# Dilated attention scores as three single-rate products of split queries and keys, on each head's own 64 rows, two heads interleaved

## The reference

```python
def dilated_attention(q, k, v, positions):
    h = N_HEADS_C
    q = partial_rope_2(to_heads(q, h), positions)
    k = partial_rope_2(to_heads(k, h), positions)
    v = to_heads(v, h)
    outs, lses = [], []
    for window, dil in DILATED_PATTERNS:
        o, lse = dilated_branch(q, k, v, window, dil)
        outs.append(o)
        lses.append(lse)
    wts = jax.nn.softmax(jnp.stack(lses, axis=0), axis=0)
    o = jnp.sum(wts[..., None] * jnp.stack(outs, axis=0), axis=0)
    return from_heads(o)
```

## Time and profile before

| | us |
|---|---|
| median of 3 runs | 2215.31 |
| lowest, highest | 2212.41, 2215.72 |
| profiled execution, its own time | 2214.59 |
| its span (first to last instruction) | 2212.8 |

### The profile page before, as it was taken

How to read it: one execution, slowest core, us unless ns; L and a number is a source line. 1 busy time by engine, 2 the same in 40 slices (tenths; PEclk the granted TensorE clock), 3 DMA queues, 4 the chain that set the end, 5 groups by cost and what they waited for, 6 DMA issues and landing times.

```text
span 2212.8 us, 33023 instructions
## 1 busy us (share of the span) xinstructions
PE 2160.8 (98%) x12331; PEld 1840.0 (83%) x12331; DVE 1500.5 (68%) x2224; ACT 944.2 (43%) x1882; POOL 1189.3 (54%) x582
## 2 busy tenths in 40 slices
PE   6999999999999999999999999999999999999997
PEld 4788888877899988887887898888897887888885
DVE  6834877554666692897646776677896728777676
ACT  3254663011556610644743555412555725455311
POOL 4747403776477677745016644577653037444673
PEclk9999999999999999999999999999999999999999
DMA  8422102422133333232002222322221012222221
GB/s 318 156 73 86 62 30 88 181 94 96 58 115 115 109 142 135 77 115 77 1 4 92 96 91 100 115 95 84 107 93 61 1 39 86 92 90 115 95 95 57
DMA packets 32776, 206.78 MB, mean 93 GB/s; under 512 B 4080, under 2 KB 4336, under 8 KB 11632
## 3 DMA queue, kind: packets, MB, share of 16 engines
q1 hardware_dynamic: 32192, 200.27, 24.9%
q10 hardware_dynamic: 432, 4.46, 0.5%
HBM read 202.61 MB, written 2.10 MB: 93 GB/s over the span
## 4 chain that ended last, share of the span: by engine, by line
PE 87%; DVE 8%; DMA 1%; DVEq 1%; issue 1%; ACT 1%; POOL 1%; POOLq 0%; SPq 0%; ACTq 0%
PE PS L1118 18%; PE PS L1120 18%; PE PS L1119 18%; PE PS L1560 5%; PE PS L1572 5%; PE PS L1375 3%; PE PS L1373 3%; PE PS L1374 3%; PE PS L1586 3%; PE PS L1449 2%; PE PS L1451 2%; PE PS L1450 2%; DMA raw<-slabs_dram 1%; DVE PS L3374 1%; PE PS L1132 1%
## 5 line engine op out<-in xcount | busy, mean ns | idle before, releaser
L665 POOL TENSOR_TENSOR w_hi<-raw,zero_c 128x512 fp32r<-128x512 f32 (+1 forms) x135 | 279.5, 2088 | 546.2 <-PE PS L1120 544.8
L669 POOL TENSOR_TENSOR w_lo<-raw,w_hi 128x512 fp32r<-128x512 f32 (+1 forms) x135 | 367.4, 2740 | 5.8
L1118 PE MATMUL PS<-b_hi,w_hi 128*128 128x512 f32 x528 | 209.8, 397 | 1.0 <-POOL w_lo L888 1.0
L1119 PE MATMUL PS<-b_lo,w_hi 128*128 128x512 f32 x528 | 209.3, 396 | 0.0
L1120 PE MATMUL PS<-b_hi,w_lo 128*128 128x512 f32 x528 | 209.3, 396 | 0.0
L3288 DVE TENSOR_TENSOR b_lo<-a_all,b_hi 128x512 fp32r<-128x512 f32 x44 | 162.5, 3732 | 49.4 <-ACT b_hi L2446 49.4
L1118 PE MATMUL PS<-f_hi,w_hi 128*128 128x512 f32 x448 | 177.6, 397 | 0.7 <-DVE f_lo L2590 0.7
L1120 PE MATMUL PS<-f_hi,w_lo 128*128 128x512 f32 x448 | 177.6, 396 | 0.0
L1119 PE MATMUL PS<-f_lo,w_hi 128*128 128x512 f32 x448 | 177.6, 396 | 0.0
L688 POOL TENSOR_TENSOR w_lo<-raw,w_hi 128x512 fp32r<-128x512 f32 x48 | 71.0, 1479 | 93.6 <-ACT w_hi L2438 93.6
L1118 PEld LDWEIGHTS PS<-b_hi,w_hi 128*128 128x128 f32 x528 | 99.5, 188 | 25.6 <-POOL w_lo L888 1.2
(11 more groups left out here) (570 smaller groups left out, 6822.3 us busy)
## 6 DMA issues: line engine op xcount, KB each, us to landing
raw<-slabs_dram SPq DMA_DIRECT2D x161, 1024.0 KB, 4.8
aux<-ada_dram SPq DMA_DIRECT2D x18, 512.0 KB, 5.0
ada_first<-ada_dram SPq DMA_DIRECT2D x11, 512.0 KB, 13.9
cmpw<-cmpw_dram ACTq DMA_DIRECT2D x2, 2048.0 KB, 11.7
ada_late<-ada_dram SPq DMA_DIRECT2D x8, 512.0 KB, 3.3
ada_last<-ada_dram SPq DMA_DIRECT2D x8, 512.0 KB, 5.8
xT<-xT_dram SPq DMA_DIRECT2D x1, 2048.0 KB, 9.2
out_dram<-t SPq DMA_DIRECT2D x4, 512.0 KB, 2.7
```

The lines of the kernel that those rows point to most:

```text
L665: high = nc.gpsimd.tensor_tensor(w_hi[:, slot, c], raw[:, slot, c], zero[:, 0:c.stop - c.start], ALU.add)
L669: low = nc.gpsimd.tensor_tensor(w_lo[:, slot, c], raw[:, slot, c], w_hi[:, slot, c].bitcast(f32), ALU.subtract)
L1118: nc.tensor.matmul(out, a_hi_, b_hi_, start=start, stop=False)
L1119: nc.tensor.matmul(out, a_hi_, b_lo_, start=False, stop=False)
```

## The change

The queries of two heads are now one transposed tile without zeros, kept as high and low part (`T2_split`), and so are the keys (high part in `T2a`, low part in `z2_split`, over the keys' own place). A job names the 64 rows that are its own (`rows`). Three single-rate products of 64 rows (high x high, high x low, low x high) give a score tile. Two heads that share a tile (`mate`) take their score tiles together: at an even step TensorE issues six matmuls, head A and head B by turns, into two banks, and at the odd step none. Tiles of one key block are computed 256 columns wide (`wide = max(2, nb)`); the second half is not read. The two heads' outputs lie side by side in one bank and are divided together, after the second one's last product (`finishes`). In the eight turns at steps 3 to 38 ScalarE now takes the high part and VectorE, in the same step, the low part, which waits for ScalarE's (`turned_act`). The high parts of the outputs lie in two places instead of one (`o_high`).

```diff
@@ -353,8 +353,10 @@
         t4 = at("t4", 81920, [P, KD + 1, SEQ])
+        z2_split = at("z2_split", 32768, [P, 6, TT, 512], f32r)
         T2 = at("T2", 0, [P, 16, SEQ])
-        T2a = at("T2a", 57344, [P, 8, SEQ])
+        T2_split = at("T2_split", 0, [P, 16, SEQ], f32r)
+        T2a = at("T2a", 57344, [P, 4, SEQ], f32r)
...
-        o_hi = at("o_hi", 57344, [P, KD, SEQ], f32r)
+        o_hi_far = at("o_hi_far", 57344, [P, 4, SEQ], f32r)
+        o_hi_near = at("o_hi_near", 0, [P, 4, SEQ], f32r)
...
+                self.together, self.home, self.prior, self.finishes = {}, [None] * len(jobs), {}, {}
-                tiles, m = [], 0
+                tiles, m, mates, last_in = [], 0, 0, {}
                 while m < len(jobs):
-                    group = [m + 1, m] if m + 1 < len(jobs) and is_pair(jobs[m + 1]) else [m]
+                    woven = m + 1 < len(jobs) and is_pair(jobs[m + 1])
+                    group = [m + 1, m] if woven else [m, m + 1] if jobs[m]["mate"] else [m]
+                    for i, g in enumerate(group):
+                        if jobs[m]["mate"]:
+                            self.home[g] = (6 + mates % O_BANKS, TT * HD * i)
+                        else:
+                            self.home[g] = (6 + g % O_BANKS, 0)
+                        self.prior[g] = last_in.get(self.home[g][0], 0)
+                        self.finishes[g] = () if jobs[g]["mate"] else (g - 1, g) if jobs[m]["mate"] else (g,)
+                    for g in group:
+                        last_in[self.home[g][0]] = g + 1
+                    mates += jobs[m]["mate"]
                     for j in (3, 0, 2, 1):
+                        at0 = len(self.scores)
                         for g in group:
                             for c in range(len(jobs[g]["q"])):
-                                self.scores.append((g, c, j, len(group) > 1))
+                                self.scores.append((g, c, j, woven))
                             tiles.append((g, j, len(self.scores) - 1))
+                        if jobs[m]["mate"]:
+                            self.together[at0] = (at0, at0 + 1)
+                        else:
+                            for i in range(at0, len(self.scores)):
+                                self.together[i] = (i,)
                     m += len(group)
...
-        dilated_q = [T2[:, (12 if h % 2 == 0 else 4) + h // 2, :] for h in range(8)]
+        dilated_q = [(T2_split[:, 12 + i, :], T2_split[:, 4 + i, :]) for i in range(4)]
+        dilated_k = [(T2a[:, i, :], z2_split[:, 4, :, 128 * i:128 * i + 128]) for i in range(4)]
...
-            two_jobs.append(job(dilated_q[h], T2a[:, h // 2, :],
+            two_jobs.append(job((dilated_q[h // 2],), dilated_k[h // 2],
                                 lambda kb, h=h: z2[:, 5, kb, 64 * h:64 * h + 64],
-                                O2[:, :, 64 * h:64 * h + 64], strip2[:]))
+                                O2[:, :, 64 * h:64 * h + 64], strip2[:],
+                                rows=(slice(64 * (h % 2), 64 * (h % 2) + 64),), mate=h % 2 == 0))
...
+        def split_turn(src, homes, scale):
+
+            hi, lo = homes
+            return (src, P, [(hi, scale)], [(lo, scale, hi)])
...
-        two_turns += [apart(i, two_src(3, 128 * i), dilated_q[2 * i:2 * i + 2], halves) for i in range(4)]
-        two_turns += [whole(i, two_src(4, 128 * i), P, T2a[:, i, :], 1.0) for i in range(4)]
+        two_turns += [split_turn(two_src(3, 128 * i), dilated_q[i], -HD ** -0.5) for i in range(4)]
+        two_turns += [split_turn(two_src(4, 128 * i), dilated_k[i], 1.0) for i in range(4)]
...
+        def o_high(i):
+            return o_hi_far[:, i, :] if i < 4 else o_hi_near[:, i - 4, :]
...
-                    if step < n:
+                    for i in plan.together.get(step, ()):
+                        m = plan.scores[i][0]
...
+                        if i >= s_banks:
+                            pe.wait_ge(scores_masked, g0 + i - s_banks + 1)
+                    if step in plan.together and jobs[plan.scores[step][0]]["rows"] is None:
...
-                            pe.wait_ge(scores_masked, g0 + step - s_banks + 1)
                         nc.tensor.matmul(PS[:, step % s_banks, 0:128 * nb], query_tile(jobs[m]["q"][c], j),
                                          jobs[m]["k"][:, 128 * lo:128 * (lo + nb)], start=True, stop=True
                                          ).then_inc(scores_ready, 1)
+                    elif step in plan.together:
+                        for part, (of_q, of_k) in enumerate(((0, 0), (0, 1), (1, 0))):
+                            for i in plan.together[step]:
+                                m, c, j, _ = plan.scores[i]
+                                lo, nb = key_range(jobs[m], j)
+                                rows_, wide = jobs[m]["rows"][c], max(2, nb)
+                                last = nc.tensor.matmul(PS[:, i % s_banks, 0:128 * wide],
+                                                        key_tiles(jobs[m]["q"][c][of_q], rows_, j, 1),
+                                                        key_tiles(jobs[m]["k"][of_k], rows_, lo, wide),
+                                                        start=part == 0, stop=part == 2)
+                                if part == 2:
+                                    last.then_inc(scores_ready, 1)
...
-                        if v in plan.first and m >= O_BANKS:
-                            pe.wait_ge(out_used, m0 + m - O_BANKS + 1)
+                        if v in plan.first and plan.prior[m]:
+                            pe.wait_ge(out_used, m0 + plan.prior[m])
+                        bank, col0 = plan.home[m]
                         for b in range(nb):
-                            last = nc.tensor.matmul(PS[:, 6 + m % O_BANKS, 64 * j:64 * j + 64],
...
-                            m = plan.values[v][0]
                             dve.wait_ge(pv_done, v0 + v + 1)
-                            finish(jobs[m], m, plan.sums[m][0] % 8)
+                            for m in plan.finishes[plan.values[v][0]]:
+                                finish(jobs[m], m, plan.sums[m][0] % 8, plan.home[m])
...
-                o = PS[:, 6 + m % O_BANKS, 0:TT * HD].rearrange("p (t d) -> p t d", t=TT)
+                o = PS[:, home[0], home[1]:home[1] + TT * HD].rearrange("p (t d) -> p t d", t=TT)
...
                 def two_taken(n):
                     _, _, _, dves = two_turns[n]
-                    if dves:
+                    if n < HEAD and dves:
                         dve.wait_ge(turned, turn0 + n + 1)
-                    for dst, scale in dves:
-                        V.tensor_scalar(dst, laid(PS[:, n % 4 if n < HEAD else 3, :], dst), scale, None, ALU.mult
-                                        ).then_inc(turned_dve, 1)
+                    if n >= HEAD:
+                        dve.wait_ge(turned_act, act0 + counts[n][0])
+                    for dst, scale, *rest in dves:
+                        if rest:
+                            V.scalar_tensor_tensor(out=dst, in0=laid(PS[:, 3, :], dst), scalar=scale,
+                                                   in1=laid(rest[0].bitcast(f32), dst), op0=ALU.mult, op1=ALU.subtract
+                                                   ).then_inc(turned_dve, 1)
+                        else:
+                            V.tensor_scalar(dst, laid(PS[:, n % 4, :], dst), scale, None, ALU.mult
+                                            ).then_inc(turned_dve, 1)
```

50 lines of the change are left out of this document (27 added, 23 removed).

## The result

The changed kernel takes **2233.5 us** (2232.5 to 2235.5) against 2213.9 for the kernel before (four runs; the 2215.3 above is the median of three): 1.0084 times as long, with an interval of 1.0072 to 1.0097. It is 19.7 us slower, where 12 us faster was forecast. In the profiled execution (2235.5 us) TensorE is busy for 97% of the span, VectorE for 67%: a little less of a bound than in the earlier trace rows.

What follows compares the result with a forecast made beforehand. The prediction took TensorE, busy for 98% of the span, as the bound. It summed 19.0 - 1.7 - 2.4 - 2.6 = 12.3 us gained, so 2214.6 - 12.3 + 0.7 = 2203 us, with a range from 2197 to 2215.

Steps and rivals of the forecast that it cites:

- scores, six matmuls at a time: Dilated steps: two heads' scores side by side fall from 4.32 to 1.94 us, 19.0 us gained over eight pairs.
- full windows of ScalarE and VectorE: Third pair of dilated heads: TensorE's work falls below ScalarE's 10.57 us, so 0.87 is lost twice, 1.7 us.
- joint division: Dilated steps: dividing both heads at once makes TensorE wait 0.3 us a pair, eight times, 2.4 us.
- VectorE's wait in the turns: First 48 steps: VectorE's subtraction waits for ScalarE's high part, delaying masks; 1.3 us a layer, 2.6 us in all.
- second rival: Heads side by side, but each of 64 shape changes exposes 0.162 us, 10.4 us in all; 2209 us, chance 0.15.
- estimate of 2.5 us for a pair of heads: Dilated scores: if two row tiles reach the skill page's share of their ideal, 1.54 times, 2.5 us a pair.
- the other waits for two banks: Dilated steps away from the joint division: one mask of at most 0.69 us against two steps of TensorE's work, costing nothing.
- what is given back in the dilated steps: Three terms: full windows 1.7 us, joint division 2.4 us, TensorE's end of the attention nothing.
- the price of the turns: First 48 steps: eight turns a layer priced between nothing and 3.2 us, 1.3 taken, from 0.4 us late at step 14.
- last sentence: Signs of a wrong prediction: row halves taken in turn, VectorE's wait reaching TensorE in full, or a later stage waiting elsewhere.
- The slower rival: Dilated scores: heads one after the other, with exposed tails at shape changes; 9.5 us lost, 2225 us, chance 0.09.

Runs made afterwards that it cites:

- e6: e5 plus the joint division of two heads, each tile still in its own step: 2223.5 us.
- e8: The changed kernel with VectorE's low parts one step later and each head divided by itself in three of four pairs: 2229.8 us.
- e5: The kernel before with only the dilated tiles of two heads by turns, f32 scores and old turns kept, separate division in three of four pairs: 2225.7 us.
- e9: The changed kernel with VectorE's low parts one step later and a one-block value product issued 5 and 10 times in steps 64 and 65: 2224.7 us.
- e14: e13 plus the one-block value product issued 5 and 10 times in steps 64 and 65: 2220.2 us.
- e3: The changed kernel without pairing: each head's three 64-row products in its own step, each head divided alone: 2237.2 us.
- e12: e5 with ScalarE instead of VectorE copying the four-block tile of every second dilated head: 2218.4 us.
- e16: The kernel before with ScalarE instead of VectorE copying the four-block tile of every second dilated head: 2215.0 us against 2214.2.
- e1: The new schedule alone: f32 scores and old turns, two heads' tiles issued together at even steps and divided together: 2228.6 us against 2214.2 before.
- e7: e5 plus both heads' tiles issued together at the even step: 2225.4 us.
- e15: e14 with ScalarE taking all four-block copies of the dilated heads: 2218.9 us.
- e13: The changed kernel with VectorE's low parts one step later and ScalarE copying every second dilated head's four-block tile: 2222.2 us.
- e17: e15 with VectorE's scaling of the differential heads at step 66 instead of 64: 2228.0 us.
- e18: e15 with the differential heads' square root at step 66, scaling at 69 and the last four output transpositions 5, 5, 5 and 1 steps later: 2230.6 us.
- e4_full_rows: The changed kernel with all 128 rows in each of the six products of an even step, scores not the reference's: 2234.8 us.

## Why the prediction was wrong

The sum was 19.0 - 1.7 - 2.4 - 2.6 = 12.3 us gained; 19.7 were lost.

| step of the prediction | forecast | measured |
|---|---|---|
| scores, six matmuls at a time | 19.0 gained | 6.5 us of TensorE's time, of little use in this order |
| full windows of ScalarE and VectorE | 1.7 back | not the limit (ScalarE 36.7 of 58.0 us) |
| joint division | 2.4 back | nothing (e6, e8) |
| VectorE's wait in the turns | 2.6 back | 7.7 by the windows; one step later gives 4.5 to 5.9 back |
| the order by turns | nothing | 10.5 lost (e5) |
| the granted clock | not thought of | 2 to 4 lost (e9, e14) |

**What held.** Two heads do run side by side, at no cost at all (e3). Of the prices weighed for it, the one of the second rival (side by side, with a price at each change of shape) was right in kind and nearly in size: 0.162 us a change or 0.32 a visit forecast, 0.39 measured. The prediction gave it 0.15 and forecast without it. The Trainium skill, TensorE: Matmul & The Clock Gate, Part 3 (Packing small matmuls), led to an estimate of 2.5 us for a pair of heads; the four tiles took 0.90 + 0.55 + 0.72 + 0.55 = 2.72. That agrees in size but not in cause, since all over 1.94 stands at the ends of a visit and none inside.

**The step that failed first** is the sentence "the other waits for two banks fall on steps where one mask ... stands against two steps of TensorE's work, and cost nothing", and with it the whole section on what is given back in the dilated steps. It took one engine's queue against TensorE's work, step by step, at the place where the division is, and let every other step stand as it was. But the change had moved the tiles: the wide ones next to each other. By e5, e12 and e16, the circle through all three engines (score, mask, exponential, transposition, copy, and back to the mask behind the copy) holds TensorE up where wide tiles meet, and the order before kept them apart. The runs showed 10.5 us lost by the order, a term that the sum doesn't have. The profile before had the signs. ScalarE and VectorE both waited (17.4 and 17.9 us in a layer's attention, in which TensorE was busy for 97%), so each lag was just covered; and the earlier trace rows shows a copy of 0.69 us with a mask of 0.68 at its back. What was missing was to write the new order down with the durations of the earlier trace rows for a whole pair of heads and follow who releases whom.

**The second** is the price of the turns: "between nothing and 8 x 0.4 = 3.2 us" a layer; it was 3.85. The upper end was no bound, since it was worked out at one step for one waiting instruction. At step 14 VectorE stood for 1.73 us, because ScalarE's high part comes behind its exponentials, and three masks (1054.50, 1054.70, 1054.91) and not one were behind it. Of this the prediction's own last sentence was right: it is wrong "if VectorE's new wait reaches TensorE in full at each turn".

**The slower rival** had a chance of 0.09 and another mechanism (the row halves one after the other). No rival put the order in question, so the loss of e5_order, over half of all, lay in no case, and the range ended 18.5 us below the result.

**How the parts add up.** From before: order 10.5 (e5); the two tiles at once and the joint division, nothing apart, 4.0 more together (e1, 14.5), which the spread of e1 and e5 hardly separates: at full clock a layer's dilated steps take 57.15 us in e1, 57.12 and 57.20 in e7 and 56.9 in e5, and 2.3 is the clock of e1's other layer. The turns and the new products together are the last 5.2 of 19.7. The turns alone are 7.7 by the windows, so the products gave back about 2.5 (an estimate, from medians that spread by more). From the other end: late low part 4.5, copies 6.8, fill 2.0, all copies 1.3; 4.7 remain.

**Why e15, with less work on TensorE than before, isn't faster than before.** In e15 TensorE is busy for 50.2 of 52.6 us, 2.7 of it the repeats (26 records of 0.104); without them it is 47.5, 2.9 less than before (50.4), so the saving is there and is spent on waits. The trace names them. In the third pair TensorE is busy for 14.03 of 14.67 us, and the repeats stand where it waited 0.87 and 1.60 us in e13 for ScalarE's copies behind the square root and its table loads. The first pair has a wait of 1.21 us for a copy of ScalarE, and two output transpositions wait 0.65 and 0.39 us for VectorE's low part of the outputs. Before, the waits of a layer were 0.44, 0.37 and 0.60 us.

**Open** is whether another place for the normalisation would take the third pair's waits away, which e17 doesn't show, and how e18 loses its time. No order was tried that keeps wide tiles apart and pairs the heads all the same (A's four blocks with B's one).

## What to carry to other kernels

When a change moves work in an order that three engines follow with fixed lags, cost the order before the work: write one period of the new order down with durations, and follow the circle of releases through every engine's queue. Two long steps that become neighbours can cost more than the bound engine gains, and the bound engine's saving is worth little until the circle is shorter than its work. An instruction that waits for another engine's result of the same step costs what stands behind it in its queue; put it a step later. And small matmuls on part of the rows should come in long visits: three products between whole-array work pay 0.39 us each time.

## What the runs showed of the hardware

- Two matmuls of 64 rows, on the two halves of the array and into two banks, take the time of one: 0.55 us for three or for six of 256 columns, 0.89 and 0.90 for 512 (e3_alone, changed kernel).
- Going from whole-array f32 work to 64-row single-rate work and back costs 0.39 us: 0.20 within the products, 0.09 at the transposition ahead and 0.10 at the value product behind (changed kernel). Going from whole-array f32 work to whole-array single-rate work and back costs nothing (e4_full_rows: 0.82 us where 0.83 is the sum).
- The granted clock fell to the lower level after 4 us in which TensorE had worked 1.53 us (the changed kernel, 1118 to 1122). 13 added f32 matmuls of 64 columns in that place (2.7 us) kept it up in one layer of e9_busy and in both of e14 and e15. The same program differed between its layers by 2.3 us (e1_sched, 0.94), 2.95 (e9_busy, 0.94) and 6.2 us (e17_norm_later, 0.86), with the clock at 1.00 in the other layer; at equal clocks the layers of one run differ by 0.5 us at most (e15_copies_act).
